# A hybrid NSA and S5 block on one core: compression weights in tiles of their own, powers and flattening in another order, half a dense block ahead of Y, a token-wise end of the output projection

## What is computed

```python
h = rmsnorm(x, norm_g)
q, kc, vc, ksl, vsl, kwi, vwi, gl, gate_nsa, u, gate_s5, mg = split(h @ w_in)
k_cmp = compress(kc, cmp_pos_k, cmp_w1_k, cmp_w2_k)      # gelu(flat @ w1) @ w2 on blocks of 32 tokens, stride 16
v_cmp = compress(vc, cmp_pos_v, cmp_w1_v, cmp_w2_v)
o_nsa = gates * (softmax(q k_cmp) v_cmp, softmax(rope(q) ksl) vsl, softmax(rope(q) kwi) vwi)
branch_a = (o_nsa * silu(gate_nsa)) @ w_proj_nsa
y = s5_scan(u, ...)                                      # complex diagonal recurrence, Re(C x) + D u
z = gelu(y); o_s5 = z * sigmoid(z @ w_glu + b_glu)
branch_b = (o_s5 * silu(gate_s5)) @ w_proj_s5
merged = sigmoid(mg_a) * branch_a + sigmoid(mg_b) * branch_b
out = rmsnorm(x + merged @ w_out, final_g)
```

## Time and profile before

| what | value |
|---|---|
| median of 3 runs | 471.16 us (469.15 to 473.84) |
| the profiled execution's own time | 476.43 us |
| its span from first to last instruction | 474.4 us |
| busy: PE, weight loads, VectorE, ScalarE, GpSimd | 431.0, 349.4, 290.3, 201.2, 154.3 us |
| mean granted TensorE clock | 0.971 of full speed |
| chain of waits, share of the span | PE 60%, VectorE 16%, ScalarE 5%, issue 3%, DMA 3%, GpSimd 1% |
| moved by DMA | 47.27 MB, mean 100 GB/s |

### The profile page before, as it was taken

How to read it: one execution, slowest core, us unless ns; L and a number is a source line. 1 busy time by engine, 2 the same in 40 slices (tenths; PEclk the granted TensorE clock), 3 DMA queues, 4 the chain that set the end, 5 groups by cost and what they waited for, 6 DMA issues and landing times.

```text
span 474.4 us, 7326 instructions
## 1 busy us (share of the span) xinstructions
PE 431.0 (91%) x2811; PEld 349.4 (74%) x2811; DVE 290.3 (61%) x645; ACT 201.2 (42%) x396; POOL 154.3 (33%) x78
## 2 busy tenths in 40 slices
PE   0999999979597998969998999999999999999991
PEld 0888888869375795646665677888888888899991
DVE  1666889999999545898999786134153070162334
ACT  5742778712125245697654642222322222233323
POOL 0342442431123401131314125544445444454420
PEclk9999999998898978999999999999999999999997
DMA  9954961221748227110101101564333334322104
GB/s 248 252 118 117 163 166 44 70 81 33 233 132 175 61 51 169 39 44 2 46 0 47 29 18 44 173 226 110 109 90 92 88 91 118 104 90 90 46 0 177
DMA packets 72738, 47.27 MB, mean 100 GB/s; under 512 B 21144, under 2 KB 69728, under 8 KB 72672
## 3 DMA queue, kind: packets, MB, share of 16 engines
q1 hardware_dynamic: 71520, 46.74, 37.6%
q10 hardware_dynamic: 1184, 0.07, 0.2%
HBM read 42.61 MB, written 4.19 MB: 99 GB/s over the span
## 4 chain that ended last, share of the span: by engine, by line
PE 60%; DVE 16%; ACT 5%; issue 3%; DMA 3%; POOL 1%; SPq 0%; DVEq 0%; ACTq 0%
PE bank L885 16%; PE bank L887 16%; PE bank L886 16%; DMA raw<-in_w_in 3%; PE bank L1154 3%; PE bank L1172 2%; PE bank L1193 2%; DVE bank L1271 2%; DVE prob L1607 2%; DVE pwt L1271 1%; DVE prob L1627 1%; PE bank L1108 1%; POOL w_lo L610 1%; DVE X L1271 1%; PE bank L1132 1%
## 5 line engine op out<-in xcount | busy, mean ns | idle before, releaser
L610 POOL TENSOR_TENSOR w_lo<-raw,w_hi 128x1024 fp32r<-128x1024 f32 (+2 forms) x57 | 137.2, 2406 | 258.3 <-ACT w_hi L638 258.3
L885 PE MATMUL bank<-hT_lo,w_hi 128*128 128x512 f32 x288 | 116.9, 406 | 6.3 <-POOL w_lo L610 6.2
L886 PE MATMUL bank<-hT_hi,w_lo 128*128 128x512 f32 x288 | 114.0, 396 | 0.0
L887 PE MATMUL bank<-hT_hi,w_hi 128*128 128x512 f32 x288 | 113.9, 396 | 0.0
L638 ACT ACTIVATE w_hi<-raw 128x1024 fp32r<-128x1024 f32 (+2 forms) x57 | 59.5, 1043 | 99.2 <-PE bank L887 78.3
L885 PEld LDWEIGHTS bank<-hT_lo,w_hi 128*128 128x128 f32 x288 | 55.1, 191 | 20.5 <-POOL w_lo L610 7.1
L887 PEld LDWEIGHTS bank<-hT_hi,w_hi 128*128 128x128 f32 x288 | 55.2, 192 | 12.0
L886 PEld LDWEIGHTS bank<-hT_hi,w_lo 128*128 128x128 f32 x288 | 55.1, 191 | 10.7
L830 ACT ACTIVATE prob<-prob,nmax 128x128 f32<-128x128 f32 (+2 forms) x64 | 35.3, 552 | 24.6 <-DVE nmax L1607 24.6
L886 PE MATMUL bank<-w_hi,m_lo 128*128 128x256 f32 x128 | 36.2, 283 | 0.0
L887 PE MATMUL bank<-w_hi,m_hi 128*128 128x256 f32 x128 | 36.2, 283 | 0.0
(11 more groups left out here) (211 smaller groups left out, 737.8 us busy)
## 6 DMA issues: line engine op xcount, KB each, us to landing
raw<-in_w_in SPq DMA_DIRECT2D x28, 512.0 KB, 3.9
raw<-in_w_in SPq DMA_DIRECT2D x16, 256.0 KB, 3.7
raw<-in_w_out SPq DMA_DIRECT2D x8, 512.0 KB, 3.4
x_sb<-in_x SPq DMA_DIRECT2D x4, 512.0 KB, 5.6
raw<-in_cmp_w_k SPq DMA_DIRECT2D x4, 512.0 KB, 4.0
raw<-in_cmp_w_v SPq DMA_DIRECT2D x4, 512.0 KB, 5.1
raw<-in_w_proj_s SPq DMA_DIRECT2D x4, 512.0 KB, 3.4
raw<-in_w_proj_nsa SPq DMA_DIRECT2D x8, 256.0 KB, 4.1
```

The lines of the kernel that those rows point to most:

```text
L610: nc.gpsimd.tensor_tensor(view(w_lo, j % NSPLIT, dims), w, view(w_hi, j % NSPLIT, dims).bitcast(F32), ALU.subtract).then_inc(lo_done, 1)
L885: nc.tensor.matmul(dst, w[0], x[1], start=first, stop=False, skip_group_check=True)
L886: nc.tensor.matmul(dst, w[1], x[0], start=False, stop=False, skip_group_check=True)
L887: return nc.tensor.matmul(dst, w[0], x[0], start=False, stop=last, skip_group_check=True)
```

## The change

**Compression weights.** The eight blocks leave the raw ring. Pieces 0 and 2 go to a tile `w1_even`, pieces 1 and 3 to `w1_odd`, each holding the k and v part of a piece. `w1_even` lies where x was and later probT is, `w1_odd` where W was. SyncE loads piece 0 behind ksl, piece 1 behind vc, piece 2 behind gs3, piece 3 behind gn0.

**Order on PE and ScalarE.** ScalarE splits gs0 right after val1 is used and gs1 before it copies V3. PE cuts gs2 and gs3 in halves: gs2's first half, HT, gs2's second half, KCMP and VCMP, gs3's first half, SCC, gs3's second half, Y. ScalarE copies hid and kcT before it takes gs2 and gs3 out of PSUM. gn0 moves from bank 1 to bank 7.

**Order on VectorE.** The powers of 4 entries come before CS and CT, `powers` multiplies real and imaginary rows in one instruction (`pwt` doubles in size), the rotation of kwi comes one scan step earlier, and so do both flattenings.

**Output projection.** Columns 0 to 511 go in 96 matmuls of 512 columns, row tile by row tile (wa0 to wa3). Columns 512 to 767 stay as they were. Columns 768 to 1023 go token tile by token tile with both weight blocks present; the second one, wo3_1, is split into `f_hi` and `f_lo`. The end of the work goes tile by tile: VectorE scales and SyncE stores columns 0 to 511, ScalarE scales columns 512 to 1023.

```diff
-    b += [(n, 1) for n in ("ksl", "kwi", "kc", "vc", "val0")]
-    for i, n in enumerate(("val1", "val2", "gs0", "gs1")):
-        b += [(n, 1), (f"w1k{i}", 0), (f"w1v{i}", 0)]
+    b += [(n, 1) for n in ("ksl", "kwi", "kc", "vc", "val0", "val1", "val2", "gs0", "gs1")]
...
-    b += [(f"wo{q}_{h}", 1) for q in range(4) for h in range(2)]
+    b += [(f"wa{n}", 1) for n in range(4)]
+    b += [(f"wo{q}_{h}", 1) for q in (2, 3) for h in range(2)]
...
-    use("gn0", 1)
+    use("gn0", 7)
...
+                   [("below_w1", [P, 4, T], F32), ("w1_even", [P, 2, 4, 256], F32)],
...
+                   [("w1_odd", [P, 2, 4, 256], F32), ("Y_sb", [P, GP, NCH], F32)],
...
+            if name == "wo3_1":
+                return [f[:, 0:2, :].rearrange("p a t -> p (a t)").rearrange("p (k n) -> p k n", n=dims[1]) for f in (f_hi, f_lo)]
...
+            def compression_weights(i):
+                if i == 0:
+                    wait_fill(sp, f"xT{KT - 1}")
+                elif i == 1:
+                    wait_fill(sp, "KR")
+                else:
+                    sp.wait_ge(compressed, i - 1)
+                for r, n in enumerate("kv"):
+                    w = a["cmp_w1_" + n][0].rearrange("(kt p) n -> p kt n", p=P)[:, 4 * i:4 * i + 4, :]
+                    sp.dma_start((w1_even, w1_odd)[i % 2][:, r], w).then_inc(w1_in[i % 2], 16)
...
+                if name in ("ksl", "vc", "gs3", "gn0"):
+                    compression_weights(("ksl", "vc", "gs3", "gn0").index(name))
...
+                sp.dma_start(out[0, P * i:P * i + P, 0:512], r_sb[:, i, 0:512]).then_inc(stored, 16)
+                sp.wait_ge(y_high_ready[i], 1)
+                sp.dma_start(out[0, P * i:P * i + P, 512:1024], r_sb[:, i, 512:1024]).then_inc(stored, 16)
...
+            after("val1")
             for i in range(NT):
+                if i == NT - 1:
+                    after("val2")
...
-            after("val1")
-            after("val2")
...
-            gate_s5(2)
             evacuate("HT", hid[:, :, :, :].rearrange("p r h n -> p (r h n)"), bk("HT")[:, 0:256])
             ac.wait_ge(kc_zero, 1)
-            gate_s5(3)
             for g in range(GROUPS):
                 rows = slice(DH * g, DH * g + DH)
                 evacuate("KCMP", kcT[rows, g, :], bk("KCMP")[rows, 0:NC])
+            for t in (2, 3):
+                gate_s5(t)
 
             def cmp_exp(m):
                 ac.wait_ge(cs_done, m + 1)
...
+            for n in range(4):
+                after(f"wa{n}")
+            for i in range(NT):
+                ac.wait_ge(r_done, i + 1)
+                square(0, i, slice(0, 512))
+            after("wo2_0")
+            after("wo2_1")
+            for i in range(NT):
+                ac.wait_ge(r_done, NT + 1 + i // 2)
+                square(1, i, slice(512, 768))
+            for i in range(NT):
+                ac.wait_ge(r_done, NT + 3 + i)
+                square(2, i, slice(768, 1024))
+                ac.wait_ge(fin_var, i + 1)
+                nc.scalar.activation(rms[:, 2, i:i + 1], rms[:, 1, i:i + 1], ACT.Sqrt).then_inc(fin_sqrt, 1)
+                ac.wait_ge(root_done, i + 1)
+                nc.scalar.activation(r_sb[:, i, 512:1024], r_sb[:, i, 512:1024], ACT.Copy, scale=rms[:, 3, i:i + 1])\
+                    .then_inc(y_high_ready[i], 1)
 
...
+                pe.wait_ge(w1_in[i % 2], 32 * (i // 2 + 1))
...
+                if i < 3:
+                    ins.then_inc(compressed, 1)
+                else:
+                    fill(ins, "H")
...
-            channel_major("gs2", "gs2")
+            channel_major("gs2", "gs2", kts=(0, 4))
...
-            channel_major("gs3", "gs3")
...
+            channel_major("gs2", "gs2", kts=(4, KT))
...
+            channel_major("gs3", "gs3", kts=(0, 4))
...
+            channel_major("gs3", "gs3", kts=(4, KT))
...
+            for n in range(4):
+                w = weights(f"wa{n}")
+                for i in range(NT):
+                    if n == 0:
+                        open_bank(pe, f"WA{i}")
+                    for kk in range(2):
+                        kt = 2 * n + kk
+                        if i == 0:
+                            pe.wait_ge(m_split, kt + 1)
+                        ins = mm3(bk(f"WA{i}")[:, :], merged(kt, i), [v[:, kk, :] for v in w], kt == 0, kt == KT - 1)
+                    if n == 3:
+                        fill(ins, f"WA{i}")
+                if n < 3:
+                    ins.then_inc(part_used, 1)
+
+            for h in range(2):
+                w = weights(f"wo2_{h}")
...
+            w = weights("wo3_0"), weights("wo3_1")
+            pe.wait_ge(r_done, NT)
+            for i in range(NT):
+                open_bank(pe, f"W3_{i}")
+                for kt in range(KT):
+                    ins = mm3(bk(f"W3_{i}")[:, 0:256], merged(kt, i), [v[:, kt % 4, :] for v in w[kt // 4]], kt == 0, kt == KT - 1)
+                fill(ins, f"W3_{i}")
...
+                while n < count:
+                    by_re, by_im = pwt[:, 0, :, 0:n], pwt[:, 1, :, 0:n]
+                    fr, fi = (dst[:, r, n - 1].unsqueeze(1).unsqueeze(1).broadcast_to((P, 2, n, GP)) for r in range(2))
+                    tt(by_re, dst[:, :, 0:n], fr, MUL)
+                    tt(by_im, dst[:, :, 0:n], fi, MUL)
+                    tt(dst[:, 0, n:2 * n], by_re[:, 0], by_im[:, 1], SUB)
+                    tt(dst[:, 1, n:2 * n], by_im[:, 0], by_re[:, 1], ADD)
+                    n *= 2
+
...
+            powers(pw_sb, ARE, AIM, CH)
...
+            rotate_k(1, rope[:, 2, :])
             run_step(3)
-            rotate_k(1, rope[:, 2, :])
+            flatten(0)
             run_step(4)
-            flatten(0)
-            run_step(5)
             flatten(1)
             build_e(True, 1)
-            for j in range(6, RUN + 1):
+            for j in range(5, RUN + 1):
                 run_step(j)
...
+            for i in range(NT):
+                residual(f"WA{i}", slice(i, i + 1), slice(0, 512))
             for m in range(2):
...
+                ve.wait_ge(fin_sq, 2 * m + 2)
+                times_gain(slice(2 * m, 2 * m + 2), slice(0, 512))
...
+            for m in range(2):
+                residual(f"W2_{m}", slice(2 * m, 2 * m + 2), slice(512, 768))
+            ve.wait_ge(fin_sq, 2 * NT)
+            times_gain(slice(0, NT), slice(512, 768))
+
+            for i in range(NT):
+                residual(f"W3_{i}", slice(i, i + 1), slice(768, 1024))
+                ve.wait_ge(fin_sq, 2 * NT + i + 1)
+                link(V.tensor_reduce(rms[:, 0, i:i + 1], ssq4[:, i:i + 1, 0:3], AX_X, ALU.add))
+                variance(fin_var, i, i + 1)
+                times_gain(slice(i, i + 1), slice(768, 1024))
+                ve.wait_ge(rg_done, 4 + i)
+                inverse_root(fin_sqrt, i + 1, i, i + 1, root_done)
+                V.tensor_scalar(r_sb[:, i, 0:512], r_sb[:, i, 0:512], rms[:, 3, i:i + 1], None, MUL).then_inc(y_ready[i], 1)
```

182 lines of the change are left out of this document (68 added, 114 removed).

## The result

The changed kernel takes 458.67 us (median of 4 runs, 458.34 to 459.13). The kernel before, in 4 runs beside it, takes 472.50 (469.15 to 474.52). The ratio is 0.969, 95% interval 0.965 to 0.974: 13.8 us less. The forecast was 455.0, range 449 to 461: the measured time lies inside the range, 3.7 above the point. The profiled executions are 459.13 and 476.43, so 17.3 less, where the forecast's sum had 16.6.

The account below looks back on a forecast made before the run. PE, busy 91%, was taken as the bound, then VectorE's scan at Y. 14.0 us up to attention plus 2.6 at the output projection made 16.6; off the median 471.16 that gave 454.6, stated as 455, range 449 to 461.

Parts of the forecast that it names:

- PE up to Y: Before Y, PE's waits (12.6 us) and slow clock behind them (6.5) go: 19.1, PE ready for Y at 148.1.
- slow-clock term: Before Y, 6.5 us of low granted clock behind PE's gaps would be given back when the waits go.
- VectorE: Up to the scan's end: powers edit gains, lead capped at 4.7 by ScalarE's states, 2.4 left; scan done at 155.1.
- The new wait: At Y: PE, ready at 148.1, would wait about 7 us for VectorE's scan.
- Y and behind: Y starts 12.0 us earlier and takes 7.7; 11.4 left at the e_cmp transposes, 14.0 behind the first scores.
- gn0's bank: First scores: moving gn0 to bank 7 removes their wait, 1.6 us net plus 1.0 for the clock.
- Output projection: Projection and tail: fewer matmuls save 1.2 us, the tail 1.7, a new wait costs 0.3: 2.6, bounds 1.0 and 3.5.
- Taking the 16.6 off the median: Final step: the 16.6 us sum subtracted from the median 471.16, not the profiled 476.4, giving 454.6, stated as 455.
- (b): Before Y: scan not in the way, VectorE keeps its whole 4.7 us or more; 451.6, down to 448; chance 0.12.
- (c): Attention: the lead is lost there and no clock comes back; 459.6, up to 462; chance 0.17.
- (d): Before Y: weight loads delay PE; with 12 us of such waits, 460 to 467; chance 0.09.
- (e): From Y on: the 7 us gap leaves the clock at half and it stays; 472 and above; chance 0.04.

Follow-up runs that it names:

- e12: The kernel before, unchanged, run again for a second trace: median 474.9 us, its profiled execution 471.88 us.
- e1: Changed kernel with the powers put back behind CS and CT, six instructions a doubling: 462.88 us.
- e5: e2 with ScalarE splitting gs3 behind the two Gelus of hidn, so GpSimd's low part of gs3 starts later: 455.53 us.
- e2: Changed kernel with only the order of the early scan steps (kwi rotation, flattenings) put back as before: 458.61 us.
- e10: Changed kernel with gn0 back in bank 1, nothing else: 460.93 us.
- e9: Changed kernel with the output projection and the end behind it as in the kernel before: 461.92 us.
- e3: Changed kernel without steps 7 and 8 of the scan within runs, so its output is not the layer's: 451.12 us.

## Where the prediction was right and where wrong

- **PE up to Y: right.** Ready for Y at 148.1 was forecast; it was 148.5. Of the waits named, none is left. The size of the slow-clock term (6.5) belongs to the one profiled execution, as e12 shows.
- **VectorE: right, in parts too.** Scan done at 155.1 forecast, 155.48 measured, with PE's start 0.34 later, so the lead was 2.4, as forecast. The two low parts of GpSimd were missed; e1 shows them hit again, and Y then 3.4 later. The scan's second step waited 0.45 for ScalarE's states, the cap of 4.7. The kwi rotation started at 91.40 and lost 1.8 (0.85 of wait, and 1.67 for a product of 0.70; 2.0 forecast), which e5 gave back once the copy of X was out of GpSimd's way. That this copy stands so close to a third low part, e2 alone showed.
- **The new wait: right.** About 7 forecast, 7.17 measured.
- **Y and behind: 1.1 too much.** Y started 11.5 earlier, not 12.0, took 7.9, not 7.7, and gn0 waited 0.43 for ScalarE's copy of Y out of bank 7: the move to bank 7 has this small price. The transposes came 10.3 earlier, forecast 11.4. Against that the first scores ran at full clock: 13.6 earlier at the end of attention, forecast 14.0.
- **gn0's bank: right.** 2.6 forecast with the clock, 2.3 in e10.
- **Output projection: 0.9 too little.** 2.6 forecast, 3.5 by the traces, 3.3 in e9. The matmuls gave 0.7 (0.9 forecast: the 256-column ones were priced at 0.120 us, while the row has 203 of them in 24.00 us, 0.118), PE's wait ahead of the last columns was 0.3 as forecast, the loop was 3.07 a tile (3.0 forecast). The term that was mis-sized is the way out: I kept the 4.3 us from the last scale to the end of the span. With half of the tile issued 0.4 us ahead and 256 KB transfers, ScalarE's scale ends at 454.45 and the span 2.85 later. Which of the two, the earlier issue or the smaller transfer, gives how much was not tested.
- **The sum: right, in part by luck.** 16.6 forecast, 17.3 against the profiled execution. The end of attention came 0.4 short and the output projection 0.9 over, and the two errors partly cancel.
- **The step that failed is the last: "Taking the 16.6 off the median".** The sum was read from one execution of 476.4 with clock losses of its own. Taken off that execution it gives 459.8, and the changed kernel measured 459.13 in its profiled execution and 458.67 in the median: 0.7 and 1.1 off. Taken off the median of three runs it gives 454.6, 4.1 off, since those three were 3.5 below the median of all 43. 474.7 less 16.6 would be 458.1, though the 43 were taken in four sets and the changed kernel in one. So most of the 3.7 by which the forecast of 455 is too low has nothing to do with the change, and the range took it in. The three runs' own spread of 4.7 us, at one and the same schedule, was the sign of it.
- **Rivals.** (b) falls: VectorE did not keep its 4.7. (c) is near in time (459.6), but not in mechanism: the lead reached the end of attention whole, and e3 shows 6.2 more would have. (d) falls: no wait for compression weights. (e) falls: the clock was back before Y ended.
